# A delta-net head's short convolution, done token by channel: tokens shifted over partitions by DMA instead of transposed on PE

## The reference

```python
DN_HEADS, DN_HEAD_DIM, SHORT_CONV, SEQ = 16, 128, 4, 256
h = rmsnorm(x, g_pre[i])
proj = h @ w_in[i]
qkv, z_a, b_raw, a_raw, glu_in, z_b, gate_logits = jnp.split(proj, _split_points(), axis=-1)
qkv = jax.nn.silu(causal_depthwise_conv(qkv, w_conv_qkv[i]))   # y[t] = sum over k of w[k] * x[t - 3 + k]
q, k, v = jnp.split(qkv, 3, axis=-1)
q, k, v = l2norm(heads(q)), l2norm(heads(k)), heads(v)
o_a = gated_delta_chunked(q, k, v, g_log, beta)
```

## Time and profile before

| what | value |
|---|---|
| median of the runs | 2145.78 us |
| time of the profiled execution | 2146.13 us |
| its span, from the first to the last instruction | 2144.3 us |
| PE, DVE, ACT, POOL busy | 2118.7, 1486.1, 1240.2, 336.7 us |
| clock granted to TensorE | 0.999 of full speed |
| DMA | 439.71 MB, mean 205 GB/s |

### The profile page before, as it was taken

One profiled execution on the slowest core, in us unless ns is written; L12 is line 12 of the kernel. 1 busy time (PEld: TensorE's weight loads), 2 busy tenths in 40 slices (PEclk: granted clock), 3 DMA queues, 4 the chain that ended last, 5 costly groups with the idle time before them and its releaser, 6 DMA issues.

```text
span 2144.3 us, 29098 instructions
## 1 busy us (share of the span) xinstructions
PE 2118.7 (99%) x10009; PEld 1753.2 (82%) x10009; DVE 1486.1 (69%) x2758; ACT 1240.2 (58%) x2396; POOL 336.7 (16%) x456
## 2 busy tenths in 40 slices
PE   8999999999999999999999999999999999999998
PEld 6888888888888888888888877887888888888886
DVE  5877777788999986568665564643666745556666
ACT  6666666677777865457455554553454555555543
POOL 2111111147666642010000000000000000000000
PEclk9999999999999999999999999999999999999999
DMA  8777667678877866676776665565665556554462
GB/s 260 205 207 210 198 191 203 188 216 246 247 206 216 226 203 218 206 246 209 262 254 238 235 201 195 191 194 164 205 228 201 187 184 196 184 170 138 158 215 99
DMA packets 430627, 439.71 MB, mean 205 GB/s; under 512 B 27424, under 2 KB 302112, under 8 KB 428336
## 3 DMA queue, kind: packets, MB, share of 16 engines
q1 hardware_dynamic: 412640, 380.78, 57.4%
q0 software_dynamic: 7744, 35.98, 5.0%
q10 hardware_dynamic: 10128, 21.50, 2.7%
HBM read 410.92 MB, written 27.28 MB: 204 GB/s over the span
## 4 chain that ended last, share of the span: by engine, by line
PE 87%; DVE 8%; issue 1%; ACT 1%; POOL 1%; DMA 0%; SPq 0%; DVEq 0%; ACTq 0%; POOLq 0%
PE pair L462 26%; PE pair L464 25%; PE pair L463 25%; DVE w_lo L443 3%; DVE QB L1067 2%; PE QA L1518 1%; PE RA L1534 1%; PE RA L624 1%; POOL acc_p L1036 0%; PE QB L1603 0%; PE RA L800 0%; PE RA L1760 0%; PE RB L1760 0%; PE pair L484 0%; PE pair L482 0%
## 5 line engine op out<-in xcount | busy, mean ns | idle before, releaser
L443 DVE TENSOR_TENSOR w_lo<-raw,w_hi 128x512 fp32r<-128x512 f32 x1368 | 920.2, 692 | 404.2 <-ACT w_hi L436 403.4
L436 ACT ACTIVATE w_hi<-raw 128x512 fp32r<-128x512 f32 x1368 | 828.2, 625 | 459.4 <-PE pair L464 454.3
L462 PE MATMUL pair<-w_hi,in_hi 128*128 128x512 f32 x2336 | 935.9, 401 | 3.4 <-DVE in_lo L1135 2.8
L464 PE MATMUL pair<-w_hi,in_lo 128*128 128x512 f32 x2336 | 911.5, 390 | 0.0
L463 PE MATMUL pair<-w_lo,in_hi 128*128 128x512 f32 x2336 | 909.9, 390 | 0.0
L464 PEld LDWEIGHTS pair<-w_hi,in_lo 128*128 128x128 f32 x2336 | 438.4, 188 | 93.5
L462 PEld LDWEIGHTS pair<-w_hi,in_hi 128*128 128x128 f32 x2336 | 439.1, 188 | 90.9 <-DVE in_lo L1135 3.3
L463 PEld LDWEIGHTS pair<-w_lo,in_hi 128*128 128x128 f32 x2336 | 439.4, 188 | 86.6 <-issue 1.0
L1036 POOL TENSOR_TENSOR acc_p<-acc_p,tap 128x256 f32<-128x256 f32 x160 | 184.3, 1152 | 38.6 <-ACT tap L1010 25.2
L1010 ACT ACTIVATE tap<-upad,cwl 128x256 f32<-128x256 f32 x192 | 96.8, 508 | 51.2 <-POOL acc_p L1036 50.2
L1067 DVE SCALAR_TENSOR_TENSOR QB<-upad,cwl,QB 128x256 f32<-128x256 f32 x272 | 119.6, 479 | 0.0
(11 more groups left out here) (442 smaller groups left out, 1895.7 us busy)
## 6 DMA issues: line engine op xcount, KB each, us to landing
raw<-in_w_in_dram SPq DMA_DIRECT2D x512, 256.0 KB, 3.9
raw<-in_w_in_dram SPq DMA_DIRECT2D x80, 1024.0 KB, 5.1
raw<-in_w_out_dram SPq DMA_DIRECT2D x48, 1024.0 KB, 5.0
raw<-in_w_kv_shared_dram SPq DMA_DIRECT2D x24, 1024.0 KB, 5.1
raw<-in_w_br_a_dram SPq DMA_DIRECT2D x16, 1024.0 KB, 6.5
raw<-in_w_br_b_dram SPq DMA_DIRECT2D x16, 1024.0 KB, 6.5
raw<-in_w_mem_kv_dram SPq DMA_DIRECT2D x16, 1024.0 KB, 4.9
raw<-in_w_ple_gate_dram SPq DMA_DIRECT2D x16, 1024.0 KB, 5.0
```

Source lines behind the costliest of these rows:

```text
L436: act.activation(piece(blk, q)[0], raw[:, u, q % UK], ACT.Copy).then_inc(hi_ready[u], 1)
L443: dve.tensor_tensor(lo, raw[:, u, q % UK], hi.bitcast(F32), ALU.subtract).then_inc(lo_ready[u], 1)
L462: pe.matmul(o, xh, wh, start=(q == 0), stop=False)
L464: mm = pe.matmul(o, xl, wh, start=False, stop=(q == KC - 1))
```

## The change

The head stays token by channel from the projection to tok. Both packs of transposes and the copies behind them go, and with them the short convolution's rows among those that are transposed in block 0. Instead:

- The tap of the token itself is proj times its weights (qkv_new, POOL), since tokens lie on partitions and a tap's weights now run along the columns. For the tap of one token earlier, three DMAs on ACT's queue copy proj one partition further down, into by_one: 112 partitions, then 15, then the one row that passes from the first tile to the second (shift_act). POOL multiplies by_one with its weights (qkv_tap) and adds it to qkv_new.
- DVE makes the other two taps as a pair: qkv_old = proj times the weights of tap 1, plus by_one times the weights of tap 0. Three more DMAs copy the sum two partitions further down (by_two), and DVE adds it to POOL's sum (qkv_sum). ACT takes the tanh, DVE the silu into tok.
- The weights come to each partition as one row of 1536 numbers per head (wt, two buffers, 768 KB each written to SBUF), loaded by SP behind the raw weights of block h. The host lays them out so. SP's loop is written out.
- The scaling of a head moves from half step 1 to 6 on DVE, its transposes on PE from 6 to 10, keys times queries from 9 to 13, the copies of the result on ACT from 7 to 11, the store from 16 to 19.
- The new buffers lie where the second branch's buffers lie later, so their zeroing waits for the last head, and SP's first load of the second branch's bias too.

```diff
+    spot[0] = at_a
+    by_one = sb("by_one", [P, TT, QKV])
+    by_two = sb("by_two", [P, TT, QKV])
+    qkv_new = sb("qkv_new", [P, TT, QKV])
+    qkv_tap = sb("qkv_tap", [P, TT, QKV])
+    wt = sb("wt", [P, 2, SHORT, 3, P])
...
-    def keys_pe(pe, h, hs):
-        if hs == 3:
-            pe.wait_ge(psum_free, BLK_A + h + 1)
-            reach(pe, s["tok_ready"], h)
-            for c in range(3):
-                bank = QB[:, 0:S] if c == 2 else QA[:, c * S:(c + 1) * S]
-                for tile in range(TT):
-                    mm = pe.transpose(bank[:, tile * P:(tile + 1) * P], proj[:, tile, c * P:(c + 1) * P], ident)
-            mm.then_inc(s["qkv_cols"], 1)
-        if hs == 19:
-            pe.wait_ge(s["silu_done"], h + 1)
-            for tile in range(TT):
-                for c in range(3):
-                    mm = pe.transpose((QA, QB)[tile][:, c * P:(c + 1) * P], conv[:, c, tile * P:(tile + 1) * P], ident)
-            mm.then_inc(s["qkv_tokens"], 1)
+    def weight(par, k):
+        return wt[:, par, k].rearrange("p c n -> p (c n)").unsqueeze(1).broadcast_to([P, TT, QKV])
+    def taps_in_sp(sp, h, par):
+        sp.dma_start(wt[:, par].rearrange("p k c n -> p (k c n)"), t["w_conv_qkv"][h].partition_broadcast(P))\
+          .then_inc(s[f"wt_in{par}"], 16)
+    def shift_act(act, to, src, n, done):
+        act.dma_start(to[16:P, :, :], src[16 - n:P - n, :, 0:QKV]).then_inc(done, 16)
+        act.dma_start(to[n:16, :, :], src[0:16 - n, :, 0:QKV]).then_inc(done, 16)
+        act.dma_start(to[0:n, 1], src[P - n:P, 0, 0:QKV]).then_inc(done, 16)
     def keys_act(act, h, par, hs):
         if hs == 0:
             act.wait_ge(psum_ready, h + 1 + BLK_A)
-            reach(act, s["qkv_cols"], h)
+            reach(act, s["one_in"], 48 * h)
             reach(act, s["z_gated"], h)
+            reach(act, s["taps_on_dve"], 4 * h - 3)
+            reach(act, s["taps_on_pool"], 3 * h - 2)
             act.activation(proj[:, 0], pairs[par][:, 0], ACT.Copy, scale=x_rms[:, 0:1])
             act.activation(proj[:, 1], pairs[par][:, 1], ACT.Copy, scale=x_rms[:, 1:2]).then_inc(psum_free, 1)
         if hs == 1:
             act.wait_ge(psum_free, BLK_A + h + 1)
+            if isinstance(h, int) and h == 0:
+                act.wait_ge(s["pads_ready"], 4)
+            reach(act, s["taps_on_dve"], 4 * h - 2)
+            reach(act, s["taps_on_pool"], 3 * h - 1)
+            shift_act(act, by_one, proj, 1, s["one_in"])
             act.activation(z_th[:, :, :], proj[:, :, 3 * P:4 * P], ACT.Tanh, scale=0.5).then_inc(s["z_tanh"], 1)
-        if hs == 5:
-            act.wait_ge(s["conv_filled"], h + 1)
-            act.wait_ge(s["cw_staged"], h + 1)
-            reach(act, s["qkv_tokens"], h)
-            for c in range(3):
-                ins = act.activation(conv[:, c], conv_in[:, c, 0:S], ACT.Copy, scale=cw[:, 0, c:c + 1])
-            ins.then_inc(tap_done, 1)
         if hs == 14:
-            act.wait_ge(tap_done, SHORT * h + SHORT)
-            act.activation(conv_th[:, :, :], conv[:, :, :], ACT.Tanh, scale=0.5).then_inc(s["conv_tanh"], 1)
-        if hs == 20:
-            act.wait_ge(s["qkv_tokens"], h + 1)
-            reach(act, s["tok_scaled"], h)
-            act.activation(tok[:, 0].rearrange("p c n -> p (c n)"), QA[:, 0:3 * P], ACT.Copy)
-            act.activation(tok[:, 1].rearrange("p c n -> p (c n)"), QB[:, 0:3 * P], ACT.Copy)\
-               .then_inc(s["tok_ready"], 1)
-        if hs == 21:
+            act.wait_ge(s["taps_on_dve"], 4 * h + 3)
+            shift_act(act, by_two, qkv_old, 2, s["two_in"])
+        if hs == 24:
+            act.wait_ge(s["taps_on_dve"], 4 * h + 4)
+            reach(act, s["tok_ready"], h)
+            act.activation(qkv_th[:, :, :], qkv_sum[:, :, :], ACT.Tanh, scale=0.5).then_inc(s["conv_tanh"], 1)
+        if hs == 28:
             act.wait_ge(s["tok_ready"], h + 1)
             reach(act, s["scal_ready"], h)
             for tile in range(TT):
...
     def keys_pool(pool, h, par):
...
+        pool.wait_ge(psum_free, BLK_A + h + 1)
+        pool.wait_ge(s[f"wt_in{par}"], 8 * h + (16 - 8 * par))
+        reach(pool, s["taps_on_dve"], 4 * h)
+        pool.tensor_tensor(qkv_new[:, :, :], proj[:, :, 0:QKV], weight(par, 3), ALU.mult).then_inc(s["taps_on_pool"], 1)
         reach(pool, s["decay_diff"], h - 1)
         reach(pool, s["tok_scaled"], h - 1)
-        reach(pool, tap_done, SHORT * h)
         pool.tensor_copy(hst[:, par], head_all[:, bass.ds(h, 1)].rearrange("p a n -> p (a n)"))\
             .then_inc(s["head_staged"], 1)
-        taps = chan[:, CH_SHORT:CH_LONG].rearrange("p (k c h) -> p k c h", k=SHORT, c=3)
-        pool.tensor_copy(cw[:, :, :], taps[:, :, :, bass.ds(h, 1)].rearrange("p k c a -> p k (c a)"))\
-            .then_inc(s["cw_staged"], 1)
+        pool.wait_ge(s["one_in"], 48 * h + 48)
+        pool.tensor_tensor(qkv_tap[:, :, :], by_one[:, :, :], weight(par, 2), ALU.mult).then_inc(s["taps_on_pool"], 1)
+        pool.wait_ge(s["taps_on_pool"], 3 * h + 2)
+        pool.tensor_tensor(qkv_new[:, :, :], qkv_new[:, :, :], qkv_tap[:, :, :], ALU.add).then_inc(s["taps_on_pool"], 1)
         pool.wait_ge(s["norms_summed"], 4 * h + 4)
...
             dve.wait_ge(s["z_tanh"], h + 1)
             dve.scalar_tensor_tensor(z2[:, :, :], z_th[:, :, :], 1.0, proj[:, :, 3 * P:4 * P], ALU.add, ALU.mult)\
                .then_inc(s["z_gated"], 1)
-        if hs == 4:
-            dve.wait_ge(s["qkv_cols"], h + 1)
-            dve.tensor_copy(conv_in[:, 0:2, SHORT - 1:SHORT - 1 + S], QA[:, :].rearrange("p (c n) -> p c n", c=2))
-            dve.tensor_copy(conv_in[:, 2, SHORT - 1:SHORT - 1 + S], QB[:, 0:S]).then_inc(s["conv_filled"], 1)
-        if hs in (7, 10, 13):
-            k = (hs - 4) // 3
-            dve.wait_ge(tap_done, SHORT * h + k)
-            for c in range(3):
-                ins = dve.scalar_tensor_tensor(conv[:, c], conv_in[:, c, k:k + S], cw[:, k, c:c + 1], conv[:, c], ALU.mult, ALU.add)
-            ins.then_inc(tap_done, 1)
+        if hs == 3:
+            dve.wait_ge(psum_free, BLK_A + h + 1)
+            dve.wait_ge(s[f"wt_in{par}"], 8 * h + (16 - 8 * par))
+            reach(dve, s["two_in"], 48 * h)
+            dve.tensor_tensor(qkv_old[:, :, :], proj[:, :, 0:QKV], weight(par, 1), ALU.mult).then_inc(s["taps_on_dve"], 1)
+        if hs == 11:
+            dve.wait_ge(s["one_in"], 48 * h + 48)
+            reach(dve, s["tok_ready"], h)
+            dve.tensor_tensor(qkv_sum[:, :, :], by_one[:, :, :], weight(par, 0), ALU.mult).then_inc(s["taps_on_dve"], 1)
         if hs == 12:
+            dve.wait_ge(s["taps_on_dve"], 4 * h + 2)
+            dve.tensor_tensor(qkv_old[:, :, :], qkv_old[:, :, :], qkv_sum[:, :, :], ALU.add).then_inc(s["taps_on_dve"], 1)
+        if hs == 13:
             dve.wait_ge(s["z_gated"], h + 1)
             reach(dve, s["ap_stored"], 32 * (h - 1))
             dve.tensor_tensor(ex[:, par, EX_ZS:EX_ZS + S].rearrange("p (t n) -> p t n", t=TT), z2[:, :, :], both(half_g[:, :]),
                               ALU.mult)
-        if hs == 16:
+        if hs == 23:
+            dve.wait_ge(s["two_in"], 48 * h + 48)
+            dve.wait_ge(s["taps_on_pool"], 3 * h + 3)
+            dve.wait_ge(s["taps_on_dve"], 4 * h + 3)
+            dve.tensor_tensor(qkv_sum[:, :, :], qkv_new[:, :, :], by_two[:, :, :], ALU.add).then_inc(s["taps_on_dve"], 1)
+        if hs == 26:
             dve.wait_ge(s["conv_tanh"], h + 1)
-            dve.scalar_tensor_tensor(conv[:, :, :], conv_th[:, :, :], 1.0, conv[:, :, :], ALU.add, ALU.mult)\
-               .then_inc(s["silu_done"], 1)
+            reach(dve, s["tok_scaled"], h)
+            reach(dve, s["norms_summed"], 4 * h)
+            dve.scalar_tensor_tensor(tok[:, :, :, :].rearrange("p t c n -> p t (c n)"), qkv_th[:, :, :], 1.0, qkv_sum[:, :, :],
+                                     ALU.add, ALU.mult).then_inc(s["tok_ready"], 1)
...
     def scores_pe(pe, h, par, hs):
-        if hs == 6:
+        if hs == 10:
             pe.wait_ge(s["tok_scaled"], h + 1)
...
             mm.then_inc(s["kq_cols"], 1)
-        if hs == 9:
+        if hs == 13:
             pe.wait_ge(s["kq_ready"], h + 1)
...
-        if hs == 7:
+        if hs == 11:
             act.wait_ge(s["kq_cols"], h + 1)
...
-        if hs == 16:
+        if hs == 19:
             act.wait_ge(s["ap_ready"], h + 1)
...
     def scores_dve(dve, h, par, hs):
-        if hs == 1:
+        if hs == 6:
...
         load_heads(sp, 1, COL_A, 1)
         decays_sp(sp)
-        with sp.Fori(2, HEADS) as h:
+        sp.wait_ge(s["turned"], KC // 2)
+        sp.wait_ge(s["x_ss"], 2 * TT)
+        for h in range(2):
+            taps_in_sp(sp, h, h)
+        for h in range(2, HEADS):
             load_heads(sp, BLK_A + h, COL_A, h)
+            sp.wait_ge(s["taps_on_dve"], 4 * h - 6)
+            sp.wait_ge(s["taps_on_pool"], 3 * h - 4)
...
```

(15 more changed lines are left out.)

53 lines of the change are left out of this document (28 added, 25 removed).

## The result

The changed kernel takes 2245.88 us (median of 4 runs, 2243.6 to 2246.89); the kernel before, on the same chip, 2145.81 (2145.6 to 2146.41). The ratio is 1.0462, its 95% interval 1.0449 to 1.0475: 100.1 us slower. I had forecast slower, but 2166 us with a range to 2200.

A forecast was written before the change was run, and what follows sets the result against it. PE was taken as the bound, busy 2118.7 of 2144.3 us. Per head 2.6 us of new wait less 1.33 us of packs, 16 x (2.6 - 1.33) - 0.2 = +20.1 us, gave 2166 us; range 2128 to 2200.

The forecast's parts named there:

- The packs: PE, heads: two packs of six transposes per head go, 0.67 us each, 21.4 us saved over 16 heads.
- DVE's own work costs nothing by its sum: DVE, heads: four 128x768 operations (3.8 us) replace nine tap updates (3.8 us) and two copies, so no cost.
- POOL's 128x768 operation, 1.85 us: POOL, heads: length of one wide operation, reckoned at 2.15 ns per column; upper end 2.2 us.
- The block of 1.6 us by scaling: DVE, heads: a wide POOL operation holds two-input DVE work 1.6 us, three times the 0.54 us at 256 columns.
- One POOL operation in the stretch: DVE before the scaling: on the mean one later POOL operation falls there, adding 1.6 us to PE's wait.
- Three issues in 1.05 us: ACT, after the projection copies: three DMA issues of 0.33 to 0.46 us each delay the tanh of z.
- PE waits 2.6 us per head: PE, at the scaled head's transposes: 1.0 us of wait, plus 1.6 us for one more POOL operation.
- The scalings do not stop for POOL: DVE, heads: nine scalings have one tensor input, so they run unheld, 9 x 0.2 + 0.08 us.
- POOL not stopping DVE: Rival, heads: POOL does not hold DVE for long, PE waits 0.5 us or nothing; 2124 to 2133 us, chance 0.19.
- Only the first product blocking: Rival, heads: POOL's other two operations miss the stretch, PE waits 1.0 us per head; 2140 us, chance 0.10.
- The long loop: Rival, heads: slow shift landings make POOL's next head late, blocks of 28.4 us; 2203 us, chance 0.18 including full DMA engines.
- DMA engines full: Rival, heads: 1.57 MB more per head fills the DMA engines; no cost by itself, longer landings, counted within 0.18.

The follow-up runs named there:

- run 15: Changed kernel with POOL's three operations on DVE, scaling at half step 1, early tap weights, tanh of z first, turns and scores' steps later: 2131.38 us.
- run 1: Changed kernel with 20 more unread 128x512 matmuls per head on PE, just ahead of its wait for the scaled columns: 2217.56 us.
- run 9: Changed kernel with scaling at half step 1 and SP's first two tap weight loads ahead of the decays' transfers: 2152.62 us.
- run 5: Changed kernel with only DVE's scaling moved back from half step 6 to half step 1: 2156.78 us.
- run 3: Changed kernel with ACT's tanh of z ahead of the first shift's three DMA issues instead of behind them: 2222.1 us.
- run 4: Kernel before with three unread 128x768 POOL operations per head added, nothing else changed: 2214.73 us.
- run 2: Changed kernel with POOL's three operations per head cut to 8 of 384 columns in each token tile: 2162.21 us.
- run 16: Changed kernel with POOL's two products and sum done on DVE at half steps 7, 16 and 18, nothing else changed: 2169.81 us.

## Why the prediction was wrong

The direction and the way were right, the size was not. The step that failed is the price of PE's new wait: 2.6 us per head in my sum, 5.0 measured, with nothing in the sum for PE's half clock behind it, 2.3 more. 16 x (2.4 + 2.3) = 75 of the 80 us between forecast and result. Term by term:

- **The packs** (-21.4 us): near. Run 15 shows 1.2 us per block for 1.33, and less in all, as said there. **DVE's own work costs nothing by its sum**: right. It is 212.1 us for 9.7 blocks, 21.9 each, against 235.0 for 12.2, 19.3 each, and the 2.6 more are less than the 3.3 in which POOL held it; with all taps on DVE PE still never waits between 100 and 400 us.
- **POOL's 128x768 operation, 1.85 us**: 1.84 for the first. **The block of 1.6 us by scaling**: right for w_lo (2.34 - 0.69 = 1.65) and the mask product (1.61). "Nearly the whole POOL operation" was said too freely of the rows: 0.54 is three quarters of 0.742, while 1.65 is nine tenths of 1.84.
- **One POOL operation in the stretch**: wrong, it was two. I had by_one land between 3.5 and 4 us after its issue, from transfers out to DRAM; it took 3.1, 2.6 and 2.0. Two in the stretch were my own range's upper end, 2191 us. That is +1.6 us per head. The fit in the Trainium skill, "SBUF — State Buffer", section "The DMA setup-cost knee", by which I had estimated 2.9 us, was nearer.
- **Three issues in 1.05 us**: wrong, 2.23 (0.71, 0.91, 0.61), since I took the price from issues of flat rows. Of the 1.2 us, 0.8 reach the wait: z2 starts 4.3 us after the block's first matmul (234.16 to 238.46) where I had 3.5 (218.18 to 221.65). It comes after POOL's first product (237.7) now, so the term "z2 starts when POOL's first product ends" fell away.
- **PE waits 2.6 us per head**: 5.0. Of the 2.4 too little, 1.6 are the second operation and 0.8 the issues.
- **No term for PE's clock**: the step that is missing. 2.1 us per head by run 1, 2.3 by the timeline. Before, PE never stood still in this stage, so no row of it could show what a wait does to the matmuls behind it.
- **No term for the first head's weights**: the wait for this load was put at nothing. For the first head it held POOL 14.1 us and DVE 5.3 us, and the first block grew by 3.5 us more than the others; run 9 moves the load and takes 7.1 us off that block (33.7 in run 5, 26.6).
- **The scalings do not stop for POOL**: wrong. In run 3 three of them take 3.79 us. It cost little in the changed kernel (L670's longest is 1831 ns, its mean 298 between 90 and 400 us, its median 274), since POOL was mostly done by then. The Trainium skill, "SBUF — State Buffer", section "Who interferes with whom", says that tensor_scalar can enter a mode that takes the shared ports as well; I had used only its sentence on two inputs. Runs 3 and 4 agree with it: three scalings in 3.79 us, 0.67 alone, and two decay differences in 2.06 us, 0.48 alone.
- **Rivals.** POOL not stopping DVE falls by w_lo's 2349 ns. Only the first product blocking is the reverse of what happened. The long loop did not close: DVE waits 0.05 us per head for by_two. DMA engines full: falls by run 15, which has all the added transfers; the engines are busy to 0.93 there and PE waits for nothing.

So the mechanism was the one I had named (late scaling behind POOL's operations, runs 2, 4, 5 and 16), and the price per head was five times too small in the end: +1.3 us forecast, +6.3 measured.

## What to carry to other kernels

Before work goes from VectorE to an idle GpSimd, lay its operations over VectorE's queue up to the next point at which TensorE waits: three of 1.84 us cost 69 us on a kernel with 22% of VectorE idle, while in the changed kernel the same work on VectorE itself, 0.95 us each, brought 76 us back. Price a new wait of TensorE with the half-speed matmuls behind it, here 2 us on 5 (and none on 1.7). And keep a scaling or any feeder ahead of the work that waits for the other engines: here that was one number worth 89 us.
